# Decay columns in full precision, and a second key tile between the modulation stages, in a hybrid encoder step

## The reference

```
mod = silu(c) @ w_ada + b_ada                      # sh1, sc1, g1, sh2, sc2, g2
h = rmsnorm(x, norm_mix) * (1 + sc1) + sh1
proj = h @ w_in                                    # hq hf hi hog gq gk gv ga gb gz gate_a gate_b
cq, ck, cv = split(silu(causal_conv([gq, gk, gv], conv_w)))
q, k = l2norm(cq) * dk ** -0.5, l2norm(ck)         # per head of 128
log_a = -exp(a_log) * softplus(ga + dt_bias)       # decay, one per token and head
beta = sigmoid(gb)
S_t = a_t (I - b_t k_t k_t^T) S_{t-1} + b_t k_t v_t^T ;  o_t = S_t^T q_t
```

## Time and profile before

| | |
|---|---|
| time, median of 3 runs | 943.8 us (943.55 to 945.01) |
| the profiled execution | 943.71 us, span 941.9 us |
| PE busy | 919.7 us (98%), 9425 instructions |
| DVE, ACT, POOL busy | 670.0, 446.8, 108.2 us |
| chain of waits, by engine | PE 84%, DVE 6%, ACT 4%, issue 3% |
| granted TensorE clock, mean | 0.998 |

### The profile page before, as it was taken

How to read it: one execution, slowest core, us unless ns; L and a number is a source line. 1 busy time by engine, 2 the same in 40 slices (tenths; PEclk the granted TensorE clock), 3 DMA queues, 4 the chain that set the end, 5 groups by cost and what they waited for, 6 DMA issues and landing times.

```text
span 941.9 us, 22445 instructions
## 1 busy us (share of the span) xinstructions
PE 919.7 (98%) x9425; PEld 892.4 (95%) x9425; DVE 670.0 (71%) x1254; ACT 446.8 (47%) x824; POOL 108.2 (11%) x135
## 2 busy tenths in 40 slices
PE   6999999999999999999999999999999999999997
PEld 6999888999999999999999999899999999999996
DVE  3778878866577677477766888899334899994454
ACT  6687445424234554753323267456212666663223
POOL 0110011112020110100100002122001222220000
PEclk9999999999999999999999999999999999999999
DMA  9824233344433422326643332232323343323312
GB/s 350 267 81 143 59 99 110 109 134 120 116 103 107 131 75 69 107 62 193 179 138 91 90 90 82 76 90 78 94 85 104 104 118 93 91 79 96 90 51 96
DMA packets 146031, 104.82 MB, mean 111 GB/s; under 512 B 5153, under 2 KB 138855, under 8 KB 144779
## 3 DMA queue, kind: packets, MB, share of 16 engines
q1 hardware_dynamic: 138955, 79.16, 28.8%
q0 software_dynamic: 6352, 22.00, 7.6%
q10 hardware_dynamic: 624, 2.23, 0.6%
HBM read 100.06 MB, written 3.31 MB: 110 GB/s over the span
## 4 chain that ended last, share of the span: by engine, by line
PE 84%; DVE 6%; ACT 4%; issue 3%; DMA 1%; SPq 1%; DVEq 0%; ACTq 0%
PE G L2210 58%; PE G L2305 15%; PE R L2218 10%; PE R L2221 1%; DMA wada<-in_w_ada_s 1%; DVE sum_lo L1755 1%; DVE w_sum L1746 1%; SPq L1097 1%; DVE cy L1881 1%; DVE cy L1878 1%; ACT w_hi L1347 0%; DVE cy L1882 0%; ACT d_hi L1352 0%; DVE w_lo L1755 0%; DVE cy L1877 0%
## 5 line engine op out<-in xcount | busy, mean ns | idle before, releaser
L2210 PE MATMUL G<-h_hi,w_hi 128*128 128x272 f32 (+1 forms) x880 | 263.6, 300 | 0.2 <-DVE ff_shift L2156 0.2
L2210 PE MATMUL G<-h_lo,w_hi 128*128 128x272 f32 (+1 forms) x880 | 253.7, 288 | 0.1
L2210 PE MATMUL G<-h_hi,w_lo 128*128 128x272 f32 (+1 forms) x880 | 253.6, 288 | 0.0
L1639 DVE TENSOR_TENSOR w_lo<-raw,w_hi 128x1024 fp32r<-128x1024 f32 (+3 forms) x111 | 118.8, 1070 | 82.0 <-ACT w_hi L1252 81.3
L2210 PEld LDWEIGHTS G<-h_hi,w_hi 128*128 128x128 f32 x880 | 165.7, 188 | 3.2 <-DVE ff_shift L2156 0.4
L2210 PEld LDWEIGHTS G<-h_lo,w_hi 128*128 128x128 f32 x880 | 166.0, 189 | 0.3 <-issue 0.3
L2210 PEld LDWEIGHTS G<-h_hi,w_lo 128*128 128x128 f32 x880 | 165.7, 188 | 0.0
L1252 ACT ACTIVATE w_hi<-raw 128x1024 fp32r<-128x1024 f32 (+3 forms) x111 | 101.5, 914 | 114.0 <-PE G L2210 113.9
L2305 PE MATMUL G<-x_hi,sum_hi 128*128 128x272 f32 x288 | 83.9, 291 | 1.9 <-ACT partial L1363 1.8
L2305 PE MATMUL G<-x_hi,sum_lo 128*128 128x272 f32 x288 | 83.4, 290 | 0.0
L2305 PE MATMUL G<-x_lo,sum_hi 128*128 128x272 f32 x288 | 82.9, 288 | 0.0
(11 more groups left out here) (335 smaller groups left out, 2117.4 us busy)
## 6 DMA issues: line engine op xcount, KB each, us to landing
raw<-in_w_in SPq DMA_DIRECT2D x48, 512.0 KB, 4.1
raw<-in_w_up SPq DMA_DIRECT2D x44, 512.0 KB, 4.0
w_ada<-in_w_ada_t POOLq DMA_DIRECT2D x49, 256.0 KB, 3.1
wada<-in_w_ada_s SPq DMA_DIRECT2D x8, 1024.0 KB, 14.2
raw<-in_w_down SPq DMA_DIRECT2D x14, 384.0 KB, 3.5
raw<-in_w_down SPq DMA_DIRECT2D x16, 320.0 KB, 3.1
raw<-in_w_out SPq DMA_DIRECT2D x8, 512.0 KB, 4.2
w_ada_t<-in_w_ada_t POOLq DMA_DIRECT2D x15, 256.0 KB, 3.1
```

The lines of the kernel that those rows point to most:

```text
L1639: dve.tensor_tensor(lo, raw[:, i % RAW, 0:job.nk, 0:job.m], hi.bitcast(F32), ALU.subtract).then_inc(w_lo_done, 1)
L2210: ins = pe.matmul(out, w, x, start=(job.first and k == 0 and p == 0), stop=(job.last and k == job.nk - 1 and p == 2))
```

## The change

The job `gagb` is taken out. Its weights (8 columns) are loaded straight into a padded tile of 32 columns, `gab_w`, without splitting. Step `gab` j multiplies the two chunks of stage j in full precision: the moving operand is `val`, a quarter of the tokens goes to each of the four column groups, and all four stages add up in one bank of `R`. `h1` of the next stage waits for `gab`, since it writes over `val`. ACT copies the bank, and `gab_sum` brings the four quarters together by products with a constant `gate_select` (73,728 bytes, a new load). Key tile gk1 becomes the second tile between the stages: both key tiles are multiplied in step `part`, and their results leave at the end of the stages. gk1's load moves between the loads of stages 2 and 3, and its split in front of `h1` 1. `ada_T` counts as three bank uses in the first three stages, so that the bank of `gab` is skipped. The steps inside the query jobs are put in a new order.

The core of the diff (left out: the tiles' places in memory, the removed branches for `gagb`, POOL's waits, the copies of `gab` and `gab_sum` on ACT, the building of `gate_select`):

```diff
-    do("split", 0)
-    do("split", 1)
+    GK0, GK1, GQ0, GQ1 = range(4)
+    do("split", GK0)
     do("ada_rows", 0)
     do("ada_T", 0)
     do("h1", 0)
-    for j in range(1, STAGES):
-        do("ada_rows", j)
-        do("duo_part", 2 * j - 2, 0)
-        do("ada_T", j)
-        do("duo_part", 2 * j - 2, 1)
-        do("duo_part", 2 * j - 1, 0)
-        do("duo_part", 2 * j - 1, 1)
-        if j == STAGES - 1:
-            do("split_hi", 2)
-        do("h1", j)
-    do("split_lo", 2)
-    do("sel")
+    do("ada_rows", 1)
+    do("gab", 0)
+    do("part", GK0, (0,))
+    do("ada_T", 1)
+    do("part", GK0, (1,))
+    do("split", GK1)
+    do("h1", 1)
+    do("part", GK1, (0, 1))
+    do("gab", 1)
+    do("part", GK0, (2, 3))
+    do("ada_rows", 2)
+    do("part", GK1, (2,))
+    do("ada_T", 2)
+    do("part", GK1, (3,))
+    do("h1", 2)
+    do("ada_rows", 3)
+    do("gab", 2)
+    do("part", GK0, (4,))
+    do("ada_T", 3)
+    do("part", GK0, (5,))
+    do("part", GK1, (4, 5))
+    do("h1", 3)
+    do("gab", 3)
+    do("part", GK0, (6, 7))
+    do("split_hi", GQ0)
+    do("part", GK1, (6, 7))
...
-    duo(gagb, gk0)
-    around(gk1, [("g_sp",), ("split_hi", 4), ("g_a",), ("split_lo", 4)], [])
-    around(gq0, [("g_sq", 0, 2), ("g_scan",)], [])
-    around(gq1, [("g_sq", 0, 3), ("g_norm", 0, 2)], [("g_rows",), ("c_load",)])
+    mark = len(plan)
+    gk0()
+    gk1()
+    del plan[mark:]
+    do("evac", 0)
+    do("split_lo", GQ0)
+    do("gab_sum")
+    around(gq0, [("split_hi", GQ1), ("taps", 0, 0), ("taps", 0, 1), ("gab_rows",), ("split_lo", GQ1), ("evac", 1),
+                 ("sel",), ("g_sp",), ("taps", 1, 0), ("taps", 1, 1), ("g_a",)], [])
+    around(gq1, [("g_scan",), ("g_sq", 0, 2), ("g_sq", 0, 3), ("g_norm", 0, 2)], [("g_rows",), ("c_load",)])
     around(gv0, [("g_sq", 0, 0), ("g_norm", 0, 3)], [("g_bcast", 0)])
...
-        if x[0] == "conv":
+        if x[0] == "conv" and g > 1:
             at = plan.index(("evac", g)) + 1
...
+            sp.dma_start(gab_w[:, :, 0:2 * NH], t["w_in"][:, COL["gagb"]:COL["gagb"] + 2 * NH]
+                         .rearrange("(k p) m -> p k m", p=P)).then_inc(gab_in, 16)
             load(0)
-            load(1)
             for j in range(STAGES):
+                if j == 2:
+                    load(1)
                 for v in range(2):
                     sp.dma_start(wada01[:, j, v, :, :], t["w_ada_s"][j, v]).then_inc(ada_in[j], 16)
+            sp.dma_start(gab_sel[:, :, :], t["gate_select"]).then_inc(const_in, 16)
...
                 elif name == "h1":
                     dve.wait_ge(gain_ready, a[0] + 1)
+                    if a[0]:
+                        dve.wait_ge(gab_done, a[0])
...
+                elif name == "gab":
+                    j, b = a[0], first_fill[spot("gab", STAGES - 1)] % 4
...
+                    for k in (2 * j, 2 * j + 1):
+                        pe.wait_ge(val_ready, k + 1)
+                        for q in range(4):
+                            ins = pe.matmul(R[q * QUAD:(q + 1) * QUAD, b, 0:QUARTER], gab_w[:, k, :],
+                                            val[:, k % 2, q * QUARTER:(q + 1) * QUARTER], start=k == 0, stop=k == KD - 1,
+                                            skip_group_check=True)
+                    ins.then_inc(fill_done if j == STAGES - 1 else gab_done, 1)
+                elif name == "gab_sum":
+                    pe.wait_ge(ones_set, 1)
+                    pe.wait_ge(const_in, 48)
+                    wait_bank(pe, last_bank[spot("gab", STAGES - 1)])
+                    for h in range(2):
+                        fill(n, h, [mm(lambda b, q=q: R[0:QUAD + NH, b, q % 2 * QUARTER:(q % 2 + 1) * QUARTER], gab_sel[:, q, :],
+                                       gab_parts) for q in (2 * h, 2 * h + 1)])
```

More of the change, by code:

```diff
@@ L39 @@
 HALF = TOK // 2
+QUARTER = TOK // 4
 NH = 4
@@ L715, in build @@
         c_part = at("rec", "c_part", [P, 2, HK])
-        m0 = jobs[gab].m
-        w_aside = dict(rec=(at("rec", "gab_hi", [P, KD, m0], F32R, off=base + 38 * row + 512),
-                            at("rec", "gab_lo", [P, KD, m0], F32R, off=base + 38 * row + 512 + KD * m0 * 4)))
+        gab_w = at("rec", "gab_w", [P, KD, QUAD], off=base + 38 * row + 512)
+        gab_sel = at("rec", "gab_sel", [P, 4, QUAD + NH], off=base + 38 * row + 512 + KD * QUAD * 4)
+        gab_parts = sq[:, 0, 0:QUARTER]
+        w_aside = {}
         o_gate_z = at("rec", "o_gate_z", [P, 2, TOK])
@@ L1102, in _ @@
             for n, step in enumerate(plan):
-                if step[0] == "job" or step[0] == "duo" and step[1]:
+                if step[0] == "job" or step[0] == "duo":
                     for i in step[1:]:
@@ L1240, in split_weights @@
                 wait_weights(act, i)
[L1241 to L1247, removed]
                 if i in aside:
@@ L1414, in _ @@
                     read_banks(n, 0, [(ada_rows[:, a[0] % 2, :], lambda b: R[:, b, 0:P])])
+                elif name == "gab" and a[0] == STAGES - 1:
+                    read_banks(n, 0, [(gab_parts, lambda b: R[:, b, 0:QUARTER])])
+                elif name == "gab_sum":
+                    read_banks(n, 0, [(x, lambda b: R[0:QUAD + NH, b, 0:HALF]) for x in q_halves(acc[0:QUAD + NH, :])])
                 elif name == "ogate":
@@ L1533, in _ @@
                     kind, arg, _ = groups[g]
[L1534 to L1538, removed]
+                    if kind == "conv":
                         what, pair, h, slot = arg
@@ L2102, in _ @@
                     done = slot_user["dve"]
[L2103 to L2112, removed]
+                    if kind in ("pa", "pb"):
                         wait_group(dve, g)
@@ L2180, in _, with fill @@
             seen = dict(s=0, lo=0)
-            def fill(n, k, products):
+            def fill(n, k, products, banks=1):
                 f = first_fill[n] + k
@@ L2309, in _ @@
                     ins.then_inc(q_done, 1)
[L2310 to L2314, removed]
+                elif name == "part":
+                    i, ks = a
+                    if ks[0] == 0:
+                        pe.wait_ge(w_lo_done, nth_split[i] + 1)
+                    products((i, 0), (i, 1), ks=ks)
+                elif name == "gab":
+                    j, b = a[0], first_fill[spot("gab", STAGES - 1)] % 4
+                    if j == 0:
+                        pe.wait_ge(gab_in, 16)
+                        pe.wait_ge(pad_zero, 1)
+                        wait_bank(pe, last_bank[spot("x_first", N_CHUNK - 1)])
+                        assert last_bank[spot("x_first", N_CHUNK - 1)] % 4 == b
+                    for k in (2 * j, 2 * j + 1):
[5 more added lines that the diff above has]
+                    ins.then_inc(fill_done if j == STAGES - 1 else gab_done, 1)
+                elif name == "gab_sum":
+                    pe.wait_ge(ones_set, 1)
[4 more added lines that the diff above has]
+                                       gab_parts) for q in (2 * h, 2 * h + 1)])
                 elif name == "first_chunks":
@@ L2320, in _ @@
                 elif name == "duo":
-                    if a == duos[0]:
-                        pe.wait_ge(ones_set, 1)
-                        pe.wait_ge(const_in, 32)
-                    rest = range(KD - 2 if a == duos[0] else SUMS_AT, KD)
-                    products(*[(i, half) for i in a for half in range(2)], ks=rest)
+                    products(*[(i, half) for i in a for half in range(2)], ks=range(SUMS_AT, KD))
                 elif name == "vectors":
@@ L2557, in constants @@
     unit = small[:, LAST_SMALL + 1]
+    gates = np.zeros((4, QUAD, 4, QUAD + NH), np.float32)
+    for q in range(4):
+        for r in range(2 * NH):
+            gates[q, r, q, r % NH + r // NH * QUAD] = 1
     low = np.stack([m[0:QUAD, 0:QUAD].T for m in levels[:LAST_SMALL + 1]], 1)
```

53 lines of the change are left out of this document (29 added, 24 removed).

## The result

The changed kernel takes 961.3 us (median of four executions, 959.4 to 964.9) beside 944.4 for the kernel before: a ratio of 1.017, interval 1.014 to 1.020. Forecast were 957.0 us with a range of 952 to 960: slower, as foretold, by the stall foretold, but 4.3 us more than foretold and 1.3 past the end of the range. The profiled execution is the fastest of the four, 959.44 us with a span of 957.6. The slower two ran at a lower mean granted clock (0.991, 0.991, 0.987, 0.985 for 959.4, 960.3, 962.4, 964.9 us).

The account below looks back on a forecast made before the run. PE was taken as the bound nearly without a gap behind 48.28 us, ACT and DVE nearly a second bound. Profiled 943.7 + 11.1 shift + 2.5 restart = 957.3, less 0.3 of later waits: 957.0 us, range 952 to 960.

Parts of the forecast that it names:

- the stall: PE inside gq1, at the first key tile's norm, stands 13.3 us waiting for the square that DVE does after the scan.
- norm of the first key tile: On PE inside gq1: runs at 69.6 us instead of 57.94, so PE is 11.7 us later than before.
- restart: PE after the 13 us rest resumes at a lower granted clock: 2.5 us taken, bounds 0 and 2.7.
- recovered up to the inverse: The old 0.63 us wait of PE for DVE at 95.37 us disappears: 0.6 us gained.
- Rival 2: Norm inside gq1: the square is ready when PE asks, so the kernel is not slower, 941.9 us; chance 7%.
- half-length stall: Remaining case: a stall about half as long, from a misread order on ACT or DVE, near 950 us; chance 5%.
- gk0 complete at 44.4, gk1 at 45.9, the sums at 46.9: End of PE's modulation stages, in us; the first query tile then starts at 46.9 instead of 48.41.
- rival 3: Decay products: column groups don't run side by side, 6 us more on PE, time 961 us; chance 5%.
- ACT's and DVE's chain: Work behind 44.4 us: gq0's result leaves ACT at 61.6, then DVE's taps 66.7, scan 68.9, square 69.6.
- The table switch: ACT's activation table load: measured 1.28 us kept over the skill's 2.66, which would lengthen the stall 2.8 us, giving 959.8.
- rival 1: PE after the stall resumes at full pace, so the restart is free: 954.5 us; chance 17%.
- Behind it PE's work is that of before: After the stall PE stays the bound and its delay stays; only the 0.63 us at 95.37 is recovered.

Follow-up runs that it names:

- PE kept at work: Changed kernel with 56 unused products of 512 columns ahead of the first key tile's norm: 956.8 us, ratio 1.012 against the kernel before.

## Why the prediction was wrong: right in its mechanism, short in three terms

The path held: the order on DVE makes PE stand at the norm, and a stretch at half clock follows. What failed is the sum. Its decay products were too short (0.25 us a chunk for 0.37), so that everything behind them came 1.6 us late; it counted half clock behind one wait only; and it took PE's work in the inverse to be that of before, where 1.4 us were lost. The profiled execution against the forecast, as shift of PE against the kernel before:

| step | forecast | measured |
|---|---|---|
| norm of the first key tile | +11.7 | +13.28 |
| restart | +2.5 | +2.31 |
| recovered up to the inverse (117.66, before 103.25) | -0.6 | -1.18 |
| from there to the end | -0.3 | +1.4 |
| sum | +13.3 | +15.8 |

Point by point:

- *The stall* was right: 13.32 us for 13.3, at the norm, released by the square that stands behind the scan. That it agrees to 0.02 us is in part luck: PE's arrival at the norm and the square both came 1.6 us late. Rival 2 (ready in time) and the half-length stall fell with it. That it is an order of DVE's work is shown by moving the square, and then the scan.
- *"gk0 complete at 44.4, gk1 at 45.9, the sums at 46.9"* failed by 1.5 to 1.7 us: 45.9, 47.5, 48.6, so that the query tile starts 0.2 us later than in the kernel before instead of 1.5 earlier. Each of the chunks of decay products takes 0.37 us from start to next start (38.84 to 39.21, in the changed kernel's rows), not the 0.25 that I scaled from the modulation rows: 1.0 us over eight. The fourth stage's wait was 0.94 instead of 0.65; the remaining 0.3 is not itemised. Of the other waits two held, 0.90 for gk1's low part (1.0 forecast) and 0.31 for the third stage's tile (0.3); the 0.4 for the second stage's tile and the 0.4 for gq1's weights do not show. The column groups do run side by side: 0.74 us a stage, not 2. So rival 3 fell, and that its 961 is the measured median is chance.
- *ACT's and DVE's chain* held term by term; the late start passed through it one to one. gq0's result had left ACT 1.5 us late (63.1 for 61.6), and DVE's taps and scan were done 1.5 us late, the square 1.6. One term was too large, without effect: the decay rows took 1.63 us on DVE instead of 2.52.
- *The table switch*: the next activation follows the load by 1.29 us (54.40 to 55.69), so the measured figure was the right choice; the longer one would have made the stall 2.8 us longer, and it was 0.02 longer.
- *The restart* was right where I put it (2.3, 1.6 and 2.4 us in the three profiles of this order, none with PE kept at work), so rival 1 (a free restart) fell. The size was taken from PE's slow beginning, where the profile prints a granted clock of 1.00 from 7 to 13 us; that the beginning is slow by the same cause is not shown. And I counted the restart once. Waits of 1 to 2.5 us in the stages and in the inverse end in half clock too, in some executions: 959.4 us without such a fall, 963.8 with two, and with longer gaps. That this also puts the median (961.3) above the profiled execution is argued from the mean clocks; no trace shows the executions between.
- *"Behind it PE's work is that of before"* failed: the work is, its place among the instruction blocks isn't. 1.4 us are lost in the inverse, and given back, all but some 0.6, by moving the boundaries. Ahead of it 1.18 us are recovered instead of 0.6: 0.96 at the products around the old wait of 95.37, 0.2 at the later norms.

A slip without effect: the window from 48.28 begins with the first query tile, not the second.

The late start (1.6 us), the median above the profiled execution (1.9) and the loss in the inverse (1.7: 1.4 lost instead of 0.3 recovered), less the 0.6 more that was recovered, and 0.2 at the restart, make 4.4 us, beside the 4.3 by which the forecast fell short.

## What to carry to other kernels

When a bound engine gets less work in one stage, first look at when the engines behind it receive their first input: here PE had some 2 us less to do (a job of 6.0 for decay products of 3.0 and sums of 1.1), but ACT got the first key tile 5 us later (47.13 for 42.11) and the decay columns' sums 6.6 us later (48.19 for 41.59), and the order of the work behind them then made PE wait 13. Put what a wait ends on (a square of 0.7 us) ahead of what nobody waits for yet, and count a stretch at half clock as possible behind each new wait of PE. After a change of the number of instructions, read the gaps without a releaser in the dense stretches of the trace, before and after, even where the work is the same.

## What the runs showed of the hardware that was not expected

- PE's program stalls for up to 1.7 us at places 127 matmul instructions or a multiple of it apart (254 with their weight loads), where groups of 68 products of 32 columns go through in 0.83 us. Adding 24 products at the beginning of the program moved the stalls by 23 products, 100 us later. How long a stall is was not predictable: 0.32 and 1.13 us at the same place in two executions of the changed kernel.
- The granted clock fell to 0.50 behind rests of PE of 1.1 to 2.5 us, in some executions and not in others of the same kernel: behind 2.48 us at 23.6 us it fell in one profile of the changed kernel, behind 1.98 us it did not in the other.
